# Three blocks of a three-layer model on one core: the order of small steps at turn changes, in the first query and in the merge's first splits

## What is computed

```python
# window layer
q, gate = split(rmsnorm(x) @ w_in)            # 4 quads of 4 heads x 8 row tiles = 32 items
q = rmsnorm(q, g_q)                           # per head of 64
p = softmax(q @ k_band * 64**-0.5 + bias, with a sink)
x = x + ((p @ v_band) * silu(gate)) @ w_out
# third layer: 4 pairs of turns (2 FOX heads, then 1 differential head)
diff: pd = softmax(q1 k1) - lam * softmax(q2 k2);  yb = rms_norm(pd @ v) * silu(z)
merged = sigmoid(ga) * (ya @ w_branch[0]) + sigmoid(gb) * (yb @ w_branch[1])
x = x + rms_norm(merged @ w_out)
```

## Time and profile before

| | us |
|---|---|
| median of 3 runs (2331.35 to 2336.67) | 2334.31 |
| the profiled execution, its own time | 2332.58 |
| its span, first to last instruction | 2330.8 |
| TensorE busy in the span | 2245.7 (96%) |
| VectorE busy | 1116.0 (48%) |
| ScalarE busy | 874.7 (38%) |
| mean granted TensorE clock | 0.992 |

### The profile page before, as it was taken

How to read it: one execution, slowest core, us unless ns; L and a number is a source line. 1 busy time by engine, 2 the same in 40 slices (tenths; PEclk the granted TensorE clock), 3 DMA queues, 4 the chain that set the end, 5 groups by cost and what they waited for, 6 DMA issues and landing times. The chain is left out here.

```text
span 2330.8 us, 32355 instructions
## 1 busy us (share of the span) xinstructions
PE 2245.7 (96%) x11746; PEld 1794.9 (77%) x11746; DVE 1116.0 (48%) x3116; ACT 874.7 (38%) x2277; POOL 219.9 (9%) x313
## 2 busy tenths in 40 slices
PE   7999999999999998999999899999999999899998
PEld 6888888888888877777767677777777676888876
DVE  5264364353462124454554336666665666533332
ACT  4141241341352113545553234544534444522232
POOL 1000000000000001121110000010100101111123
PEclk9999999999999999999999999999999999999999
DMA  4111111111155213011134510111011102524322
GB/s 157 57 57 55 55 46 60 46 50 57 46 179 191 76 65 113 10 53 51 53 110 125 177 36 31 62 45 43 26 45 62 44 16 72 151 65 123 100 100 91
DMA packets 125012, 174.65 MB, mean 75 GB/s; under 512 B 7416, under 2 KB 73016, under 8 KB 123328
## 3 DMA queue, kind: packets, MB, share of 16 engines
q1 hardware_dynamic: 119072, 157.46, 20.3%
q10 hardware_dynamic: 5792, 15.24, 1.8%
HBM read 143.27 MB, written 29.42 MB: 74 GB/s over the span
## 5 line engine op out<-in xcount | busy, mean ns | idle before, releaser
L91 PE MATMUL heads_p_ps<-ret_w_second_hi_sb,ret_hT_hi_sb 128*128 128x512 f32 x384 | 150.5, 392 | 0.9 <-DVE ret_w_second_lo_sb L638 0.9
L91 PE MATMUL heads_p_ps<-ret_w_second_hi_sb,ret_hT_lo_sb 128*128 128x512 f32 x384 | 149.6, 389 | 0.0
L91 PE MATMUL heads_p_ps<-ret_w_second_lo_sb,ret_hT_hi_sb 128*128 128x512 f32 x384 | 149.5, 389 | 0.0
L91 PE MATMUL att_proj_ps<-br_w_second_hi_sb,br_hT_hi_sb 128*128 128x512 f32 x320 | 135.8, 424 | 1.9 <-DVE br_w_second_lo_sb L2441 1.9
L91 PE MATMUL att_proj_ps<-br_w_second_hi_sb,br_hT_lo_sb 128*128 128x512 f32 x320 | 125.5, 392 | 0.0
L91 PE MATMUL att_proj_ps<-br_w_second_lo_sb,br_hT_hi_sb 128*128 128x512 f32 x320 | 125.4, 392 | 0.0
L2390 ACT ACTIVATE br_x_sb<-br_x_sb,att_max_neg_sb 128x256 f32<-128x256 f32 (+7 forms) x128 | 97.8, 767 | 24.7 <-DVE att_max_neg_sb L2614 24.7
L91 PEld LDWEIGHTS heads_p_ps<-ret_w_second_hi_sb,ret_hT_hi_sb 128*128 128x128 f32 x384 | 72.1, 188 | 17.8 <-issue 2.5
L91 PEld LDWEIGHTS heads_p_ps<-ret_w_second_lo_sb,ret_hT_hi_sb 128*128 128x128 f32 x384 | 72.1, 188 | 15.1
L91 PEld LDWEIGHTS heads_p_ps<-ret_w_second_hi_sb,ret_hT_lo_sb 128*128 128x128 f32 x384 | 72.2, 188 | 14.6
L409 POOL TENSOR_TENSOR heads_o_rstd_sb<-heads_o_ms_sb,heads_minus_half_sb 128x1 f32<-128x1 f32 x32 | 17.6, 549 | 636.4 <-ACT heads_o_ms_sb L625 636.4
(11 more groups left out here) (558 smaller groups left out, 6331.3 us busy)
## 6 DMA issues: line engine op xcount, KB each, us to landing
early_w_kv_sb<-a_w_blocks SPq DMA_DIRECT2D x26, 1024.0 KB, 5.2
all_w_block_sb<-w_turns SPq DMA_DIRECT2D x12, 2048.0 KB, 9.0
br_y_raw_sb<-branch_yT_dram SPq DMA_DIRECT2D x32, 512.0 KB, 4.2
ret_o_dram<-early_x_rows_sb ACTq DMA_DIRECT2D x32, 256.0 KB, 2.4
all_w_block_sb<-swa_turns SPq DMA_DIRECT2D x4, 2048.0 KB, 9.2
heads_o_rows_sb<-ret_o_dram ACTq DMA_DIRECT2D x6, 1024.0 KB, 5.6
x_dram<-early_x_rows_sb SPq DMA_DIRECT2D x12, 512.0 KB, 2.9
all_w_block_sb<-a_w_blocks SPq DMA_DIRECT2D x2, 2048.0 KB, 9.3
```

The lines of the kernel that those rows point to most:

```text
L91: mm = pe.matmul(out, rows[a], w[b], start=(k == 0 and a + b == 0), stop=(k == KT - 1 and b == 1))
```

## The change

The diff, cut to its core. In the window layer:

```diff
-        LOADS = ITEMS - TILES + 2
+        FIRST_AT = 5
+        LOADS = ITEMS - TILES + 1
 pool: for s in range(TILES):
+                if s == FIRST_AT:
+                    query_factor(0)
                 key_factor(s)
-                if n <= ITEMS:          # here and on ACT and DVE: 2 <= n
+                if 2 <= n <= ITEMS:
+                    query_factor(n - 1)
 act: keys_values(t) ends with v_done; new:
+            def key_mean(t):
                 act.wait_ge(kss_done, t + 1)
                 act.activation(k_ms[:, t], k_ss[:, t], ACT.Copy, ...).then_inc(kms_done, 1)
             for s in range(TILES + 3):
+                if s == FIRST_AT + 1:
+                    query_square(0)
+                    gate_tanh(0)
+                    query_mean(0)
                 if 1 <= s <= TILES:
                     keys_values(s - 1)
                 if 2 <= s < TILES + 2:
                     copy_keys(s - 2)
+                if 1 <= s <= TILES:
+                    key_mean(s - 1)
-                if ITEMS - 1 <= n < ITEMS - 1 + AHEAD:
-                    out_high(n - ITEMS + 1)
+                if ITEMS - 2 <= n < ITEMS - 2 + AHEAD:
+                    out_high(n - ITEMS + 2)
 dve: (in the key loop query_squares(0), put_gate(0) before key_squares, norm_queries(0) behind it)
+                early_probs = t == 0
+                if early_probs:
+                    copy_probs(n - 3)
                 if 2 <= n < ITEMS + 2:
                     bias_max(n - 2)
                 ...
-                if 3 <= n < ITEMS + 3:
+                if 3 <= n < ITEMS + 3 and not early_probs:
                     copy_probs(n - 3)
 (out_low one step earlier, as out_high)
```

In the third layer `closes` is step 7 of a diff turn that another turn follows, `opens` is step 0 of the turn behind it, and `ends` is steps 6 and 7 of the last diff turn:

```diff
+SPLIT_LAST = {2: (0,), 3: (1,), 4: (2,), 5: (3,)}     # in the last turn, in place of SPLIT_STEPS
-              (TILES, 0): (TILES - 1, range(3, 6)), (TILES, 1): (TILES - 1, range(6, KT))}
+              (TILES, 0): (TILES - 1, range(3, 6)), (TILES, 1): (TILES - 1, range(6, 7)), (TILES, 2): (TILES - 1, range(7, KT))}
 pool:
+                    if opens(prev, t):
+                        inverse_root(prev, TILES - 2)
-                    if last and not last[0].fox:
+                    if last and not last[0].fox and not closes(turn, following, t):
                         inverse_root(*last)
 pe:
+                    else:                          # t == TILES
+                        transpose_probs(*last, 4)
+                        fill(t, 1)
-                    if before and not before[0].fox:
+                    if before and not before[0].fox and not opens(prev, t):
                         transpose_out(*before)
-                    fill(t, 1)
+                    fill(t, 2 if t == TILES else 1)
+                    if opens(prev, t):
+                        transpose_out(*before)
+                        probs_copied(*last)
+                        transpose_qk(*projected(turn, following, t))
                     if last:
                         values(*last)
-                    if t == TILES:
-                        merged["pe_ahead"](pe)
+                    if t >= TILES:
+                        merged["pe_ahead"](pe, t - TILES)
 act:
-                    for a in range(2):
+                    for a in (1, 0) if closes(turn, following, t) or ends(turn, following, t) else (0, 1):
                         (exp of probs[a])
                         split_high(following or GATES, range(4, KT))        # t == 0
+                    if opens(prev, t):
+                        mean_square(prev, TILES - 2)
 (copy_out(before) of an opening step: behind exps; mean_square(last) not in a closing step)
 act_ahead: rows_high(0) in step 6; branches_high in two parts in step 7; sigmoid of tile 0 first in step 8;
            rows_high(1) at the end of step 8
 dve:
+                def divide_last(t, last, clamp_first):
+                    dve.wait_ge(exp_done, turn.tiles(t + 1) * 2 - 1)
+                    (reciprocal of the second sum, lam_recip, scaling of second: mix1)
+                    if clamp_first: clamp_rows(*last)
+                    dve.wait_ge(exp_done, turn.tiles(t + 1) * 2)
+                    (reciprocal of the first sum, mix)
+                    if not clamp_first: clamp_rows(*last)
+                    if opens(prev, t):
+                        split_low(following or GATES, range(4, 7))
                     if t < TILES:
                         logits(t)
+                    if closes(turn, following, t):
+                        split_low(following.next(), SPLIT_STEPS[t - 1])     # no longer ahead of logits(7)
                     (copies of the probabilities)
+                    if opens(prev, t):
+                        norm_factor(prev, TILES - 2)
+                        out_rows(prev, TILES - 2)
+                        split_low(following or GATES, range(7, KT))
+                        dve.wait_ge(y_done, prev.number(TILES, TILES - 1))
 dve_ahead: rows_low(0) in step 6 behind silu_z; branches_low in step 8 behind the copies;
            rows_low(1) in step 8 between clamp_rows and norm_factor
 sync_ahead (step 9): loads of rows 2 and 3, each behind y_lo, ahead of the store of tile 7
 merge, chunk 0: rows_high(2), rows_low(2) in step 0, no sigmoid in step 0, branches(1) already done by pe_ahead in step 9
```

More of the change, by code:

```diff
@@ L1958, in steps, with closes, ends, split_steps @@
             return TILES if following else TILES + 2
+        def closes(turn, following, t):
+            return not turn.fox and following and t == TILES - 1
+        def ends(turn, following, t):
+            return not turn.fox and not following and t in (TILES - 2, TILES - 1)
+        def split_steps(following):
+            return SPLIT_STEPS if following else SPLIT_LAST
+        def opens(prev, t):
+            return t == 0 and prev and not prev.fox
         last_fox, last_diff = Turn(True, None, PAIRS - 1), Turn(False, None, PAIRS - 1)
@@ L2417, in turn_act @@
                         copy_gate(*last)
+                    if not following and t == TILES - 2:
+                        merged["act_ahead"](act, 0)
+                    if not following and t == TILES - 1:
+                        merged["act_ahead"](act, 2)
                     if t < TILES:
                         exps(t)
+                    if opens(prev, t):
+                        copy_out(*before)
                     if last:
@@ L2423, in turn_act @@
                         copy_gates(TILES - 1)
+                        merged["act_ahead"](act, 4)
                     if done:
                         copy_qk(*done)
-                    if t in SPLIT_STEPS:
-                        split_high((following or GATES).next(), SPLIT_STEPS[t])
-                    if last and not last[0].fox:
+                    if t in split_steps(following):
+                        split_high((following or GATES).next(), split_steps(following)[t])
+                    if last and not last[0].fox and not closes(turn, following, t):
                         mean_square(*last)
@@ L2614, in logits @@
                     dve.tensor_scalar(max_neg[:, b, :], row_max[:], -SCALE, None, ALU.mult).then_inc(neg_done, 1)
+                def divide_last(t, last, clamp_first):
+                    b = t % 2
+                    first, second = (probs[:, b, a, 0:(t + 1) * P] for a in range(2))
+                    dve.wait_ge(exp_done, turn.tiles(t + 1) * 2 - 1)
+                    dve.reciprocal(p_recip[:, b, 1:2], p_sum[:, b, 1:2]).then_inc(second_recip, 1)
+                    dve.wait_ge(second_recip, turn.number(1, t - TILES + 3 if clamp_first else 1))
+                    dve.tensor_tensor(lam_recip[:], p_recip[:, b, 1:2], lam_neg[:], ALU.mult).then_inc(lamr_done, 1)
+                    dve.wait_ge(lamr_done, turn.number(TILES, t + 1))
+                    dve.tensor_scalar(second, second, lam_recip[:], None, ALU.mult).then_inc(mix1_done, 1)
+                    if clamp_first:
+                        clamp_rows(*last)
+                    dve.wait_ge(exp_done, turn.tiles(t + 1) * 2)
+                    dve.reciprocal(p_recip[:, b, 0:1], p_sum[:, b, 0:1]).then_inc(recip_done, 1)
+                    dve.wait_ge(recip_done, turn.tiles(t + 1))
+                    dve.wait_ge(mix1_done, turn.number(TILES, t + 1))
+                    dve.scalar_tensor_tensor(first, first, p_recip[:, b, 0:1], second, ALU.mult, ALU.add).then_inc(mix_done, 1)
+                    if not clamp_first:
+                        clamp_rows(*last)
                 def divide(t, last):
@@ L2654, in turn_dve @@
                         silu_z(t)
-                        divide(t, last)
+                        if not following and t == TILES - 2:
+                            merged["dve_ahead"](dve, 0)
+                        if closes(turn, following, t) or ends(turn, following, t):
+                            divide_last(t, last, not following)
+                        else:
+                            divide(t, last)
```

(13 more changed lines are left out.)

99 lines of the change are left out of this document (57 added, 42 removed).

## The result

The changed kernel takes 2305.69 us (median of 4, 2303.87 to 2307.34) against 2334.85 before: a ratio of 0.9881, interval 0.9869 to 0.9892. Forecast were 2306.5 and a range of 2297 to 2318. The profiled execution took 2303.87 us, its span 2302.1; the span before was 2330.8, so 28.7 us are to be placed.

What follows compares the result with a forecast made beforehand. TensorE bounds the kernel, busy 2245.7 of 2330.8 us, so gains are shortened waits apart from clock. 5.8 + 2.2 + 4.9 + 6.0 + 5.1 + 3.0 = 27.0 gave 2305.6 profiled, 2306.5 median; range 2297 to 2318.

Steps and rivals of the forecast that it cites:

- Key loop and first query: Window layer: keys' mean behind their copy saves 2.5 us, first query's norm moved early saves 3.3; together 5.8, bounds 3.5 to 7.6.
- Turn changes: Steps 8, 16, 24: probabilities' copy ahead of maxima and norm saves 0.75 us each, 2.2 in all; bounds 0 to 4.5.
- Outputs: Window layer's output rows: load, high and low parts one step earlier remove four waits, saving 4.9 us; bounds 3 to 6.
- Crossings: Three changes from differential to FOX turn: reordered steps 7 and 0 save 2.3, 2.3 and 1.4 us, 6.0; bounds 3.0 to 7.8.
- Last turn's end: Last turn's end and merge's start: of 8.1 us of waits about 3.0 stays, 5.1 saved; bounds 2.5 to 7.5.
- Clock: Half-clock stretches in the key loop and two others, merge's start among them: 3.0 us saved, range 0 to 6.3.
- GpSimd's power and the second row's low part: Step 8, last turn: if VectorE's split excludes tile 7's power, y(7) comes up to 1.2 us later; otherwise nothing changes.
- The table load: Moved from merge's start to the head of step 8: priced at 1.28 us, mostly hidden; a drain could add 1.4.
- The first: Rival: the chain on VectorE and ScalarE takes the place of the waits; 13 us saved, giving 2319.6; chance 0.22.
- The second: Rival: nothing takes the waits' place and the clock stays high; 34 to 38 us, giving 2295 to 2298; chance 0.05.
- The third: Rival: slower, tile 6's chain in the opening step ends late; needs over 10.6 us lost per crossing; chance 0.02.
- The fourth: Rival: waits move on by one engine everywhere and the total stays within 0.2%; chance 0.03.

Runs made afterwards that it cites:

- query_late: The changed kernel with the first query's squares, mean, power and norm in step n = 1 again; 2310.65 us.
- window_only: The kernel before with only the changed kernel's window layer (key means, first query, early copies, outputs a step earlier); 2319.41 us.
- closer: The changed kernel with closing-step split behind silu_z, queries' norm ahead of maxima, chunk 0's gate splits at rows 5 and 6, last turn's last split in step 6; 2308.99 us.
- cross_off: The changed kernel with the three crossings from a differential to a forgetting turn (steps 7 and 0) as before; 2312.77 us.
- divide_whole: The changed kernel with the closing steps' division of the second softmax behind both exps again, as before; 2311.74 us.
- split_ahead: The changed kernel with the weight split of 0.68 ahead of the closing step's logits again; 2309.00 us.
- best_a: The changed kernel with closing-step split behind silu_z, chunk 0's gate splits at rows 5 and 6, branch weights' load at row 5, last turn's last split in step 9; 2308.21 us.
- probs_late: The changed kernel with the copy of the probabilities behind the queries' maxima and norm again at steps 8, 16, 24 and 32; 2309.62 us.
- best_b: The same as best_a, plus the second row's split behind the squares and y of tile 7 in step 8 of the last turn; 2306.05 us.

## Why the prediction was right, point by point

- **Sum.** 26.4 of the 28.7 us lie in the edited stretches (27.0 forecast), the rest is clock in code that is not changed. The median came 0.8 below the forecast. That it is so near is in part luck: the profiled execution gained 2.3 in code that is not changed, and within the 26.4 two errors cancel. The clock is 3.4 to 4.7 of them, where 3.0 stood, and the parts without it 21.7 to 23.0 (4.9 + 2.4 + 4.7 + 5.9 + 3.8 to 5.1), where 24.0 stood.
- **Key loop and first query**, 4.9 for 5.8. The order of mean and copy: 2.2 for 2.5. The query: 2.7 for 3.3 (2.6 in query_late). I had left 0.6 as a round trip; the transposes wait 0.6 for the keys' copy and the scores 0.7 for the queries'.
- **Turn changes**, 2.4 for 2.2, with the new wait of 0.4 + 0.2 named beforehand. Missed: the fourth, where the moved copy is worth 0.7 to 1.0, without which that much of the next point's gain would be lost.
- **Outputs**, 4.7 for 4.9. The step "so does their load" was wrong as a condition: a load takes 4.2, but there were 17 us, not one step, between issue and use.
- **Crossings**, 5.9 for 6.0 (window_only, without a low-clock stretch). The mechanism was right (1.7 and 0.94 of wait gone, y(6) late next), but two errors make the sum so near. I priced the new waits at 0.3 to 0.4 and they are about 0.7 on average, of which 0.26 stands at values(7), 0.25 at values(6) behind the moved split, which I had left out, and some 0.2 to 0.4 in the transposes. Against it, I put the first crossing at 1.4 because its row of before lacks the wait of 0.94; the low-clock stretch had hidden that wait, and the order is worth 1.9 there. Of the closing step I took 0.68 and 1.2 as additive; undone alone they cost 0.36 and 1.3 to 1.8.
- **Last turn's end**, 3.8 to 5.1 for 5.1. The 5.5 less a whole stretch are 3.8; but in the trace of before the slow stretch adds 1.5 to the lag behind the changed kernel and the fourth row takes 1.5 off it at once, where in window_only, with no stretch in the rows, it takes off 1.1. So the clock is between 0.4 and 1.7 of the 5.5, and these runs do not tell it closer. Wrong in any case is the step "so of 8.1 about 3.0 stays". The waits for y(7), 1.3, and at a row, 1.2 (the fourth, not the third), are there as named, and values(7) does not wait. But 4.8 stays: the 1.8 at values(5), the longest of the first row, was left out of the count, though no edit moves what makes it, the logits of tile 6 behind a split on VectorE (closer took 0.60 off it by moving that split).
- **Clock**, 3.4 to 4.7 for 3.0: 2.6 in the key loop, 0.4 in the first crossing, 0.4 to 1.7 at the end. All three stretches left the edited places; I had taken half of 6.3, since new waits might bring some back. That the places are free of them is not sure from one execution: in six of the twelve experiments one stands in one of these places (window_only, cross_off, query_late, divide_whole, split_ahead, best_a) and in probs_late one at the fourth turn change, in the changed kernel none. What I had not seen is that a stretch hides waits behind it, so that half of its busy time is more than what its going gives.
- **GpSimd's power and the second row's low part.** In the changed kernel the power of tile 7 took 1.02 while VectorE wrote the row (1967.43 to 1968.65), and 0.69 in best_b, where the row was moved away. The Trainium skill ("SBUF — State Buffer", "SBUF: two separate sides") had the power wait for the whole VectorE instruction; it ended 0.56 after the row's split did, less than the 0.69 that it takes alone, so most of its work but not all came behind the split. The trace of before has the same throughout: of its 32 powers of two columns, the 14 beside which a mix still had 0.33 to 1.14 to run took 0.89 to 1.69 and ended 0.55 to 0.56 behind the mix, each of them. The power of tile 7 cost 0.3 more here, not the 1.2 that I had given as the most, because only 0.46 of the split was left when it began.
- **The table load**, priced at its row, cost no more than that.

The timeline of the changed kernel in step 8 of the last turn, ScalarE, VectorE and GpSimd, for the last two points:

```profile
1960.55 0.20 ACT L2423 ACTIVATE att_o_ms_sb<-att_o_ssq_sb 128x2 f32<-128x2 f32 x1
...
1960.77 1.28 ACT L2975 ACT_TABLE_LOAD   x1
...
1962.06 0.63 ACT L2975 ACTIVATE br_x_sb<-br_x_sb 128x512 f32<-128x512 f32 x1
...
1967.43 1.22 DVE L3073 TENSOR_TENSOR att_m_vz_diff_sb<-br_y_raw_sb,att_m_vz_diff_sb 128x1024 fp32r<-128x1024 f32 x1 [0.71 <-ACT att_m_vz_diff_sb L2966]
...
1968.19 1.02 POOL L2126 TENSOR_TENSOR att_o_pow_sb<-att_o_ms_sb,att_minus_half_sb 128x2 f32<-128x2 f32 x1 [6.27 <-ACT att_o_ms_sb L2423]
```

The mean ends at 1960.75, the load starts at 1960.77 and the sigmoid at 1962.06: 1.28 for the whole switch. The Trainium skill ("ScalarE: Activation LUTs", "What ACT_TABLE_LOAD costs") has 2.66. The measurement decides; values(7) behind it, at 1964.18, does not wait.

- **Rivals.** The first (the chain takes the waits' place, 13 us) is refuted part by part, clock left out: crossings 5.9 where it had 3, turn changes 2.4 where it had 0, the key loop 4.9 for 4, outputs 4.7 for 3.5, the end at least 3.8 for 2.5. The second (no new wait, 34 to 38) is refuted by the new waits above. The third needed a loss of 10.6 per crossing; there is a gain of 2.0 on average. The fourth is out: the named waits went.

## What to carry to other kernels

A wait that the profile shows was worth less than its length here: 0.4 to 0.8 came back in each crossing and turn change, and the place where it comes back can be read beforehand: list what the moved instruction now stands ahead of, on its own engine, down to the next instruction that the bounding engine needs (the split ahead of the copy, the maxima ahead of the exps ahead of the queries' copy). A wait that is missing from one trace may only be hidden, by another wait ahead of it (the 1.36 of the low part ahead of the values at step 32) or by a stretch at the lower clock (block 7's low part in the first crossing). So undo the edits of an interacting pair each alone before dropping one: the fourth early copy looks idle and keeps 0.7 to 1.0 of another edit's gain. And before a difference is read, look whether a low-clock stretch stands in its place, in either trace.

## What the runs showed of the hardware that was not expected

Apart from the one at the very end, the recorded stretches at half clock lasted 3.4 to 17.1 us. One of 3.4 cost 1.7 where no wait followed, but 0.4 in the first crossing, where it hid a wait of 0.96. Two traces of kernels with the same code in a place can differ by one (at 33 us there is one in the trace of before and none in the changed one; three others have one at 16 and one at 33 us). Their sum ran from 23.9 to 40.7 us over fourteen traces, so a single trace can tell parts of over 0.3 us by shifts of the same product only where neither has such a stretch. GpSimd's power of two columns ended 0.56 behind a VectorE operation with two inputs in SBUF that had begun before it, however much of that was left, from 0.33 to 1.14. And a 512 KB load behind a 1 MB load issued 3.4 us before it took 6.6 us in place of 4.3 (in one execution of best_a).
